# Expert layer of a transformer block: 256 gathered rows of each table against both tables streamed whole through TensorE

## What is computed

```python
PEER_HEADS, N_KEYS, PEER_TOPK, PEER_BLOCK = 8, 128, 16, 128      # 16384 experts = 128 x 128 keys
def one(xb):                                                     # xb: 128 tokens x 1024
    q = (xb @ w_pq).reshape(PEER_BLOCK, PEER_HEADS, 2, PEER_DKH)
    s = jnp.einsum('thpd,hpkd->thpk', q, sub_keys)
    sv, si = lax.top_k(s, PEER_TOPK)
    cand = (sv[:, :, 0, :, None] + sv[:, :, 1, None, :]).reshape(PEER_BLOCK, PEER_HEADS, -1)
    cidx = (si[:, :, 0, :, None] * N_KEYS + si[:, :, 1, None, :]).reshape(PEER_BLOCK, PEER_HEADS, -1)
    best, pos = lax.top_k(cand, PEER_TOPK)
    eidx = jnp.take_along_axis(cidx, pos, axis=-1)
    g = jax.nn.softmax(best, axis=-1)
    act = jax.nn.gelu(jnp.einsum('thkd,td->thk', expert_u[eidx], xb), approximate=False)
    return jnp.einsum('thk,thkd->td', (g * act), expert_v[eidx])
```

## Time and profile before

| | |
|---|---|
| Time before, median of 3 runs | 1698.21 us (1697.79 to 1698.85) |
| Span of the profiled execution, first to last instruction | 1697.5 us |
| TensorE busy, VectorE busy | 86% and 75% of the span |
| HBM traffic | 436.23 MB read, mean 258 GB/s |
| Expert layer, roughly 258 to 921 us | TensorE busy 478 of 663 us, 404 GB/s |

### The profile page before, as it was taken

One profiled execution on the slowest core, in us unless ns is written; L12 is line 12 of the kernel. 1 busy time (PEld: TensorE's weight loads), 2 busy tenths in 40 slices (PEclk: granted clock), 3 DMA queues, 4 the chain that ended last, 5 costly groups with the idle time before them and its releaser, 6 DMA issues.

```text
span 1697.5 us, 22640 instructions
## 1 busy us (share of the span) xinstructions
PE 1465.2 (86%) x7548; PEld 942.4 (56%) x7548; DVE 1274.4 (75%) x2708; ACT 554.8 (33%) x1549; POOL 604.5 (36%) x611
## 2 busy tenths in 40 slices
PE   7998999896969577646648999999999999999997
PEld 2645574343435122212213797699944797699953
DVE  1687777777777777778877687489986688479985
ACT  2234334443434243323322264222201254322210
POOL 0004036777777777777774002100011002100010
PEclk9999999998989799868768999999999999999999
DMA  9885059999999999999999541275553432085141
GB/s 365 304 289 219 24 218 405 409 409 409 409 403 407 409 403 409 390 398 405 398 405 384 193 147 51 77 259 174 175 181 105 149 116 85 28 296 161 51 156 67
DMA packets 170745, 438.77 MB, mean 258 GB/s; under 512 B 12531, under 2 KB 59027, under 8 KB 170500
## 3 DMA queue, kind: packets, MB, share of 16 engines
q0 software_dynamic: 81824, 299.86, 45.1%
q1 hardware_dynamic: 88806, 137.46, 23.3%
HBM read 436.23 MB, written 1.05 MB: 258 GB/s over the span
## 4 chain that ended last, share of the span: by engine, by line
PE 58%; DMA 12%; POOL 10%; DVE 9%; issue 6%; ACT 2%; DVEq 2%; SPq 1%; ACTq 0%; POOLq 0%
PE psum L908 19%; DMA arena<-in_expert_u,indices 11%; PE psum L1313 7%; POOL arena L1497 5%; POOL arena L1490 4%; PE psum L895 3%; PE psum L914 3%; PE psum L896 3%; PE psum L939 2%; DVE arena L2532 2%; PE psum L701 2%; PE psum L1279 2%; PE psum L584 2%; PE psum L1243 2%; PE psum L681 1%
## 5 line engine op out<-in xcount | busy, mean ns | idle before, releaser
L2532 DVE CUSTOM_DVE_ANT_0 arena<-arena,psum 128x1024 f32<-128x1024 f32 x256 | 312.6, 1221 | 142.5 <-DMA arena<-in_expert_u,indices 121.9
L895 PE MATMUL psum<-arena 128*128 128x512 f32 x380 | 237.9, 712 | 184.7 <-ACT arena L1809 182.9
L1490 POOL DMA_INDIRECT arena<-in_expert_u,indices x256 | 259.6, 1014 | 93.4 <-issue 66.3
L1497 POOL DMA_INDIRECT arena<-in_expert_v,indices x255 | 246.9, 968 | 82.6 <-issue 68.6
L895 PEld LDWEIGHTS psum<-arena 128*128 128x128 f32 x380 | 68.0, 213 | 310.0 <-ACT arena L1809 289.0
L896 PE MATMUL psum<-arena 128*128 128x512 f32 x380 | 221.4, 668 | 0.0
L1432 POOL TENSOR_TENSOR small<-small 128x1 f32<-128x1 f32 (+5 forms) x30 | 32.1, 1070 | 485.4 <-DVE small L2738 191.8
L908 PE MATMUL psum<-activations_T,weight_ring 128*128 128x128 f32 x1664 | 194.5, 275 | 0.0
L908 PEld LDWEIGHTS psum<-activations_T,weight_ring 128*128 128x128 f32 x1664 | 190.3, 192 | 1.0 <-issue 0.8
L1797 ACT ACTIVATE activations_T<-activations_T 128x1 f32<-128x1 f32 x256 | 51.9, 203 | 392.9 <-DVE activations_T L2532 392.7
L896 PEld LDWEIGHTS psum<-arena 128*128 128x128 f32 x380 | 82.0, 216 | 109.7 <-issue 109.7
(11 more groups left out here) (499 smaller groups left out, 2478.3 us busy)
## 6 DMA issues: line engine op xcount, KB each, us to landing
weight_ring<-in_ffn_w_in SPq DMA_DIRECT2D x44, 1024.0 KB, 7.7
weight_ring<-in_w_in SPq DMA_DIRECT2D x14, 2048.0 KB, 9.2
weight_ring<-in_w_ada SPq DMA_DIRECT2D x8, 2048.0 KB, 11.2
arena<-in_ffn_w_out POOLq DMA_DIRECT2D x14, 1024.0 KB, 7.0
weight_ring<-in_w_out SPq DMA_DIRECT2D x6, 2048.0 KB, 8.5
weight_ring<-in_w_ada SPq DMA_DIRECT2D x16, 512.0 KB, 9.9
weight_ring<-in_w_pq SPq DMA_DIRECT2D x4, 2048.0 KB, 12.8
weight_ring<-in_ffn_w_out POOLq DMA_DIRECT2D x8, 1024.0 KB, 5.3
```

What stands on the lines that cost most here:

```text
L895: mm(o0, DIAG[:, j % ND, :], v_row(n)[:, 0:512], start=m == 0, stop=last)
L1490: nc.gpsimd.indirect_dma_start(u_row(g), None, a["expert_u"], bass.IndirectOffsetOnAxis(ap=where, axis=0)).then_inc(sem(f"u_row{g % NU}"), 16)
L1497: nc.gpsimd.indirect_dma_start(v_row(g), None, a["expert_v"], bass.IndirectOffsetOnAxis(ap=where, axis=0)).then_inc(sem(f"v_row{g % NV}"), 16)
L2532: ttr(out=u_row(n), in0=u_row(n), in1=h2, scale=1.0, scalar=0.0, op0=ALU.mult, op1=ALU.add, accum_out=DOT[:, i, m:m + 1]).then_inc(sem("u_ ...
```

## The change

The gather goes. Both tables are read from end to end, and every expert is computed for every token:

1. **First table.** 64 pairs of 128 experts (1 MB each) are loaded in four DMAs per pair, two issued by SyncE and two by GpSimd, each of which puts 256 columns of the rows on 32 partitions, in runs of 1 KB, three buffers in all. VectorE turns each block of 128 experts with one instruction of 128x1024 (`expert_block_turned`), which transposes 32x32 corners; the column order of the queries' weights and of the turned token is permuted to match. TensorE multiplies the block with all 256 tokens (8 products of 128x256), ScalarE takes the Gelu of a pair (128x512) into `S`, which holds 16384 experts x 256 tokens on chip. The last 109 of 136 search steps stand between the blocks, as do the second tile's queries and scores.
2. **Spreading.** For groups of four tokens, GpSimd forms the distances of each pick's second key to 0..127 (128x512), ScalarE makes ones of zeros with Abs and Relu, VectorE forms the weighted first-key rows (four 128x128), TensorE multiplies the two (four 128x128) and VectorE multiplies `S` with the result (128x512). 64 groups; two buffers each.
3. **Second table.** 64 loads of 1 MB by SyncE, five buffers; TensorE sums all 128 blocks for both tiles and both halves of the width (512 products of 128x512) in four banks. In the last 14 blocks the first tile goes first, so that its norm runs under the rest.
4. **Around it.** The search of the second unit and the norm of the second tile now stand ahead of the first block, and so do all four query products of the first tile. The picks are no longer shared with VectorE. The first tile's first product of the next layer, which ran among the picks, now stands behind the last block, so L939's loop runs over both tiles. Constants overwritten by the layer are loaded again. The weights of the next layer are loaded between the second table's.

```diff
+        UT = [v(BASE + n, KT, P) for n in (0, 1024, 6144)]
+        RAW = [v(0, 8, 256, of=XT), v(2048, 8, 256, of=XT), v(BASE + 4096, 8, 256)]
+        S = AR[:, END - 16384:END + 16384].rearrange("p (i t) -> p i t", t=SEQ)
+        PICKED = v(BASE + 8192, 3, SEQ)
+        SELI = v(BASE + 8960, 2, 2, PICKS)
+        ONEA = v(TRI, 2, 4, P)
+        ONEB = v(TRI + 1024, 2, 4, P)
...
+        def expert_columns(p, q):
+            return a["expert_u"][256 * p:256 * p + 256, 256 * q:256 * q + 256].rearrange("(c i) d -> i c d", i=32)
...
+            at["u"] = []
+            for p in range(EPAIRS):
+                if p in QPAIRS:
+                    queries(1, QPAIRS.index(p))
+                if p in SPAIRS:
+                    scores(1, SPAIRS.index(p))
+                if p in PICKPAIRS:
+                    picks_turned(PICKPAIRS.index(p))
+                o = bank_a()
+                for e in range(2):
+                    n = 2 * p + e
+                    pe.wait_ge(sem("ut_done"), n + 1)
+                    for k in range(KT):
+                        ins = mm(o[:, e * SEQ:(e + 1) * SEQ], UT[n % 3][:, k, :], XPT[:, k, :], start=k == 0, stop=k == KT - 1)
+                    ins.then_inc(a_full if e else sem("ut_used"), 1)
+                at["u"].append(c["a"])
+
+            at["spread"] = c["d"]
+            for g in range(GROUPS):
+                pe.wait_ge(sem("rows_ready"), g + 1)
+                pe.wait_ge(sem("columns_ready"), g + 1)
+                o = bank_d()
+                for t in range(4):
+                    ins = mm(o[:, t * P:(t + 1) * P], ONEB[:, g % 2, t, :], ONEA[:, g % 2, t, :], start=True, stop=True)
+                ins.then_inc(d_full, 1)
+            pe.wait_ge(d_free, c["d"])
+            pe.wait_ge(a_free, c["a"])
+            at["v_acc"] = c["a"]
+            experts = [PS[:, 4 + (c["a"] + n) % 4, :] for n in range(4)]
+
+            def expert_rows(n, i):
+
+                pe.wait_ge(v_sem(n // 2), v_landed(n // 2))
+                for h in range(2):
+                    ins = mm(experts[2 * i + h], S[:, ORDER[n], i * P:(i + 1) * P], v_rows(n // 2)[:, n % 2, h * 512:(h + 1) * 512],
+                             start=n == 0, stop=n == BLOCKS - 1)
+                return ins
...
-            for i in range(2):
-                o0, o1 = bank_d(), bank_d()
-                for m in range(PICKS):
-                    n = i * PICKS + m
...
-                    if n in added:
-                        continue
-                    j = summed[n]
-                    last = n == max(k for k in summed if k // PICKS == i)
-                    pe.wait_ge(sem("diag"), j + 1)
-                    pe.wait_ge(sem(f"v_row{n % NV}"), 16 * (n // NV + 1))
-                    mm(o0, DIAG[:, j % ND, :], v_row(n)[:, 0:512], start=m == 0, stop=last)
-                    mm(o1, DIAG[:, j % ND, :], v_row(n)[:, 512:1024], start=m == 0, stop=last).then_inc(sem("v_used"), 1)
-                pe.drain().then_inc(d_full, 3 if i else 2)
+            for n in range(BLOCKS - SKEW):
+                expert_rows(n, 0)
+                expert_rows(n, 1).then_inc(sem("v_done"), 1)
+            for n in range(BLOCKS - SKEW, BLOCKS):
+                ins = expert_rows(n, 0)
+            ins.then_inc(sem("v_sums"), 1)
...
+            for p in range(EPAIRS):
+                if p == 0:
+                    sp.wait_ge(a_full, at["ml_v_read"])
+                elif p == 1:
+                    sp.wait_ge(a_full, at["sc"][0, 0])
+                elif p == 2:
+                    sp.wait_ge(sem("h2_ready"), 4)
+                else:
+                    sp.wait_ge(sem("ut_done"), 2 * p - 4)
+                for q in range(2):
+                    sp.dma_start(RAW[p % 3][32 * q:32 * q + 32], expert_columns(p, q)).then_inc(sem(f"u_left{p % 3}"), 16)
+
+            def expert_load(p):
+                if p < NV:
+                    sp.wait_ge(a_full, at["u"][-1])
+                elif p < LATE:
+                    sp.wait_ge(sem("v_done"), 2 * (p - NV) + 2)
+                elif p < LATE + 6:
+                    sp.wait_ge(sem("v_done"), 64)
+                else:
+                    sp.wait_ge(sem("v_done"), 2 * (p - LATE - 6) + 104)
+                e = ORDER[2 * p]
+                sp.dma_start(v_rows(p), a["expert_v"][e * P:(e + 2) * P, :].rearrange("(c p) d -> p c d", p=P)).then_inc(v_sem(p), 16)
...
-                nc.gpsimd.indirect_dma_start(u_row(g), None, a["expert_u"], bass.IndirectOffsetOnAxis(ap=where, axis=0)).then_inc(sem(f"u_row{g % NU}"), 16)
...
-                nc.gpsimd.indirect_dma_start(v_row(g), None, a["expert_v"], bass.IndirectOffsetOnAxis(ap=where, axis=0)).then_inc(sem(f"v_row{g % NV}"), 16)
...
+            for g in range(GROUPS):
+                pool.wait_ge(a_free, at["picks", g * 4 // P])
+                if g >= 2:
+                    pool.wait_ge(sem("columns_ready"), g - 1)
+                full3 = [P, 4, P]
+                nc.gpsimd.tensor_tensor(AWAY[:, g % 2, :, :], iota.unsqueeze(1).to_broadcast(full3),
+                                        PICKED[:, 1, 4 * g:4 * g + 4].unsqueeze(2).to_broadcast(full3), ALU.subtract).then_inc(sem("away_ready"), 1)
...
+                af(S[:, 2 * p:2 * p + 2, :], o.rearrange("p (e t) -> p e t", e=2), ACT.Gelu).then_inc(a_free, 1)
...
+            for g in range(GROUPS + 1):
+                if g < GROUPS:
+                    act.wait_ge(sem("away_ready"), g + 1)
+                    af(AWAY[:, g % 2, :, :], AWAY[:, g % 2, :, :], ACT.Abs)
+                if g:
+                    if g > 2:
+                        act.wait_ge(d_full, at["spread"] + g - 2)
+                    af(ONEB[:, (g - 1) % 2, :, :], AWAY[:, (g - 1) % 2, :, :], ACT.Relu, scale=-1.0, bias=1.0).then_inc(sem("columns_ready"), 1)
                 act.drain()
...
-                act.mul(DIAG[:, j % ND, :], ident, PICKW[:, i, m:m + 1]).then_inc(sem("diag"), 1)
...
-                dve.wait_ge(sem(f"u_row{n % NU}"), 16 * (n // NU + 1))
-                dve.drain()
-                ttr(out=u_row(n), in0=u_row(n), in1=h2, scale=1.0, scalar=0.0, op0=ALU.mult, op1=ALU.add,
-                    accum_out=DOT[:, i, m:m + 1]).then_inc(sem("u_used"), 1)
-                if n - LAG in added:
-                    add_row(n - LAG)
...
+            some(searching, 11)
+            mean_of([(4, 8, VD)])
+            some(searching, 1)
+            gate(1)
+            some(searching, 6)
+            for b in range(2):
+                e = slice(b * 512, (b + 1) * 512)
+                tt(MTMP[:, b, :], full(), MODB[:, 0, e], ALU.mult).then_inc(d_free, 1)
             dve.drain()
...
+            for b in range(2):
+                e = slice(b * 512, (b + 1) * 512)
+                ins = tt(X[:, 1, e], X[:, 1, e], MTMP[:, b, :], ALU.add)
+            ins.then_inc(sem("x_ready"), 1)
+            dve.drain()
+            h2_begin(1)
+            some(searching, 2)
+            mean_of([(1, 2, D)])
+            some(searching, 1)
+            h2_end(1)
...
+            def expert_block_turned(n):
+
+                p, e = n // 2, n % 2
+                dve.wait_ge(sem(f"u_left{p % 3}"), 32 * (p // 3 + 1))
+                dve.wait_ge(sem(f"u_right{p % 3}"), 32 * (p // 3 + 1))
+                if n >= 3:
+                    dve.wait_ge(a_full if n % 2 == 0 else sem("ut_used"), at["u"][(n - 3) // 2] if n % 2 == 0 else (n - 3) // 2 + 1)
+                nc.vector.transpose(UT[n % 3].rearrange("p b (c i) -> p c b i", i=32),
+                                    RAW[p % 3][:, 4 * e:4 * e + 4, :].rearrange("p c (j b) -> p c b j", b=KT)).then_inc(sem("ut_done"), 1)
+
+            for n in range(BLOCKS):
+                expert_block_turned(n)
+                next(searching, None)
+                if n in (44, 112):
+                    pick_softmax(n // 100)
+            all_of(searching)
+
+            def spread_rows(g):
+
+                if g >= 2:
+                    dve.wait_ge(d_full, at["spread"] + g - 1)
+                dve.wait_ge(a_free, at["picks", g * 4 // P])
+                for t in range(4):
+                    n = 4 * g + t
+                    ins = ts(ONEA[:, g % 2, t, :], iota, PICKED[:, 0, n:n + 1], PICKED[:, 2, n:n + 1], ALU.is_equal, ALU.mult)
+                ins.then_inc(sem("rows_ready"), 1)
+
+            spread_rows(0)
+            spread_rows(1)
+            dve.wait_ge(a_free, at["u"][-1])
+            for g in range(GROUPS):
+                o = full().rearrange("p (t i) -> p i t", t=4)
+                s = S[:, :, 4 * g:4 * g + 4]
+                tt(s, s, o, ALU.mult).then_inc(d_free, 1)
+                if g + 2 < GROUPS:
+                    spread_rows(g + 2)
+
+            gathered(0)
```

More of the change, by code:

```diff
@@ L833, in _ @@
             at["ml_v_read"] = c["a"]
-            for _ in queries(0, 1):
-                pass
+            queries(0, 1)
+            scores(0, 1)
             o = bank_a()
@@ L1498, in _ @@
+            rsqrt(1, 0)
             for L in range(DEPTH):
```

553 lines of the change are left out of this document (191 added, 362 removed).

## The result

| | before | after |
|---|---|---|
| median of the runs (4 and 4) | 1698.53 us (1697.79 to 1699.72) | 2145.78 us (2143.39 to 2147.17) |
| profiled execution: time, span | not recorded, 1697.5 us | 2143.39, 2141.6 us |
| ratio, 95% interval | | 1.2629 [1.2611, 1.2647] |

The account below looks back on a forecast made before the run. Transfers bound the expert layer (258 to 921 us), TensorE the stage from 944 us. Start 285, first table 476, spreading 176, second table 440, then 28.5 and 753.8 sum to 2159.3; forecast 2160 us, range 2110 to 2235.

Parts of the forecast that it names:

- the first table (476 forecast, 475.0 measured): Dense products with the first table: 128 blocks x 8 products x 0.432 = 442 us, plus 34 for second-tile queries, scores, turns.
- the second (440, 440.6): Dense products with the second table: 128 blocks x 4 products x 0.858 = 439 us, plus 1 for the clock's rise.
- The 28.5 us behind them: After the second table, TensorE's 32 key and query products, 2 x 13.73 us, and a turn of 1.0 us.
- the unchanged rest: From the end of L939 to the kernel's end nothing changes: 1697.5 - 943.7 = 753.8 us.
- The start, 285: Time until the first block starts: gate 6 us later, output product, query weights, query product and scores, about 285 us.
- Output done at 264: Before the first block: output product ends 6 us after 258.0; query weights then land 12.8 us later, at 277.
- Spreading, 176: Between the tables GpSimd and ScalarE alternate: 2.7 us x 64 = 173, plus 3 to fill and empty; bounds 147 and 227.
- The transposition, 1.22: VectorE's transpose per first-table block, taken as 1.22 us from its 128x1024 with two inputs; hidden beside TensorE.
- rival (b): VectorE paces the first table through strided transposes at four times 1.22 us: +290, 2450 us; decides above 2.6; chance 0.03.
- (a): In the spreading, Abs and Relu each reload ScalarE's table, 1.28 us: period +2.6, +164, 2325 us; chance 0.03.
- (c): Loads to 32 partitions pace the first table, 15.2 us a pair: 973 in place of 476, 2657 us; chance 0.04.
- (d): Dense products of both tables take a quarter of the passes: 881 becomes 220 us, time 1499, faster; chance 0.01.

## Why the prediction was right, point by point

The direction and most of the size came from two terms that were read off rows and held: the first table (476 forecast, 475.0 measured) and the second (440, 440.6), from two records per product at the rates of the earlier trace rows. Halving either kind of product moved its stage to its half or to VectorE, so they were the bound and not just equal to it. The 28.5 us behind them held to 0.1 and the unchanged rest to 1.2 us. That the sum is as near as 17.7 us is in part luck: the start was too short and the spreading too long.

**The start, 285, was 6.8 us short, and it named the wrong limiter.** The step from "Output done at 264" to the weights at 277 and on to the first block failed. The output products began at 257.0, where the sum has them (264 less 7.13), though partly by luck: the gate was 7.6 us later and not 6, and over half of that was a wait for scores which I had no term for. They ended at 267.2, because I did not reckon that a TensorE left idle before them would be granted a lower clock; that was 3.0 us. And what ended the last wait was not the weights (278.8) but VectorE's normalisation of the second tile, L2270 (280.3), which I had no term for either. Behind it came the second tile's last turn, 1.8 us, also without a term, and the query product and scores with their hand-overs took 1.5 us more than the 8.2 in the sum. Moving the gate alone took 6.0 us off.

**Spreading, 176, was 22.8 too long.** The mechanism, GpSimd and ScalarE taking turns, is what the timeline shows. Each of its sizes was too high: GpSimd 1.04 (I took 1.2), Abs 0.53 and Relu 0.61 (1.2), hand-overs 0.04 and 0.15 (0.3): 2.37 instead of 2.7. It was also less than the whole truth. I said that VectorE's 1.8 us fits beside; it was 2.2 (143.6 us for 64 groups). The 1.8 would have held alone: without GpSimd four row operations and the product take 1.1 + 0.69 us. Beside GpSimd the four took 1.6 to 1.8 us. So the turns and VectorE lay 0.1 us apart, and taking away the turns showed it. I had put a price on VectorE held behind GpSimd only as an upper bound that added to the turns (3.5); it ran beside them. TensorE was busy two thirds of the stretch and not under half, as I had given for a sign; it paced nothing there.

**The transposition, 1.22, cost 2.035** (1.245 from neighbouring columns): the stride was what the price left out. It had no effect here: rival (b)'s point of decision was 2.6, by the halved tokens 2.8 (3.71 − 2.96 + 2.035). Had the products been cheap, this mis-sized term would have been the whole of the stage, as the 16-bit runs show.

**Rivals.** (a) No table reload stands between Abs and Relu in the timeline. (c) The transfers to 32 partitions landed in 4.7 and 5.8 us, and the stage ran with a DMA share of 0.56; ruled out. (d) did not come: the operands are all 32 bits, and every product showed two records at the forecast rate. But its price per product (a quarter) nearly held on the chip: 0.24 against 0.858 us. Its time of 1499 would not have come: with 16-bit products the second table stops at 181 us at its transfers and the first at VectorE's 364, not at 110 us each.

**Time beside the span.** The median was taken as 0.7 above the span; it lies 4.2 above: 1.8 is the time of the profiled execution beyond its own span, and 2.4 comes of its being the fastest of the four. For the kernel before, the 0.7 was the median of three runs less the span of an execution whose own time isn't on record, so it was no measure of that difference. The sum errs by 17.7 against the span, the forecast by 14.2 against the median.

## What to carry to other kernels

When a change trades traffic for arithmetic, price both per record from the trace and ask what bounds each side: here 134 MB fewer saved at most the 663 us layer, and the products alone took about 880 us in 32 bits. A dense form pays only when the products shrink with it, and then the next bounds (reads at about 420 GB/s, a transposition) must be priced too, since they stood right behind. For two engines that take turns, look at the third one's busy share before adding buffers: at 94% there was little to gain (5.5 of 153 us). Then ask what the third engine's busy time is made of: part of it was itself time spent held by GpSimd. And where an engine's program is written out in order, look at what the step just ahead of a critical one waits for.

## What the runs showed of the hardware

- VectorE's 32x32 transposition of 1024 elements per partition: 1.245 us from neighbouring 32-bit columns, 2.035 with a step of 32 bytes, 1.99 for 16-bit elements with a step of 16 bytes. With 512 words of 32 bits at a step of 16 bytes it is 1.09. In these four cases it pays per element and for the step, not per byte; turning pairs of 16-bit values as words halves it.
- VectorE's row operation of 128x128 takes 0.34 us alone and up to 1.18 us beside GpSimd's product. Taking GpSimd out of the spreading was worth 30 us of 153, of which removing the turns alone had given 5.5.
- After a wait of 3.65 us, 16 products of TensorE took 10.16 us at a mean granted clock of 0.69, against 7.13 without the wait.
- Transfers that read 1 MB, cast it and write 512 KB, issued by GpSimd, followed one another every 2.49 us from 900 to 980 us: about 420 GB/s of reads, at a DMA share of 1.12.
